# Normalising by halves of the time steps at each norm boundary, with the value tiles first in the key-value stage

## What is computed

```python
def rmsnorm(x, g):
    y = x * lax.rsqrt(jnp.mean(x * x, axis=-1, keepdims=True) + EPS)
    return y * g

x = x + short_conv_mixer(rmsnorm(x, mix_norm[0]), ...)   # stage a
x = x + conv_ffn(rmsnorm(x, ffn_norm[0]), ...)           # stage f0
kv = nsa_shared_kv(rmsnorm(x, kv_norm), ...)             # stage b
x = x + nsa_mixer(rmsnorm(x, mix_norm[1]), kv, ...)      # stage b
x = x + conv_ffn(rmsnorm(x, ffn_norm[1]), ...)           # stage f1
return rmsnorm(x, final_norm)                            # end
```

## Time and profile before

| | |
|---|---|
| median of 3 runs | 637.06 us |
| profiled execution | 636.12 us |
| its span, first to last instruction | 634.4 us |
| mean granted TensorE clock | 0.997 |
| busy: TensorE / VectorE / ScalarE / GpSimd | 97% / 77% / 63% / 8% |

### The profile page before, as it was taken

The page is one execution under the profiler, slowest core; times in us unless marked ns, Lnnn a source line. Parts: engine busy times, 40 slices in busy tenths (PEclk is TensorE's granted clock), DMA queues, the critical chain, the costliest instruction groups (busy, mean ns, idle before and its releaser), DMA issues.

```text
span 634.4 us, 11379 instructions
## 1 busy us (share of the span) xinstructions
PE 613.2 (97%) x3738; PEld 532.1 (84%) x3738; DVE 488.2 (77%) x1011; ACT 396.6 (63%) x764; POOL 53.7 (8%) x61
## 2 busy tenths in 40 slices
PE   7999999999999999999999888998999999999995
PEld 7999997888888888888989765777888888888884
DVE  4787656888888777777978799937788887777865
ACT  6645436666666566658555589827766666656644
POOL 0100011000000000011131143421000000000010
PEclk9999999999999999999999999999999999999998
DMA  8796432555655555761476300033455655555521
GB/s 304 303 334 240 168 132 100 194 204 198 201 198 198 197 179 185 295 204 41 154 247 212 123 2 2 2 100 132 136 205 197 217 205 191 177 174 189 198 100 67
DMA packets 30642, 109.56 MB, mean 173 GB/s; under 512 B 3419, under 2 KB 3691, under 8 KB 30476
## 3 DMA queue, kind: packets, MB, share of 16 engines
q1 hardware_dynamic: 30044, 106.97, 48.4%
q0 software_dynamic: 560, 2.12, 1.0%
HBM read 108.00 MB, written 1.07 MB: 172 GB/s over the span
## 4 chain that ended last, share of the span: by engine, by line
PE 88%; ACT 5%; DVE 3%; issue 2%; DMA 1%; POOL 0%; SPq 0%; DVEq 0%; ACTq 0%
PE bank L1059 26%; PE bank L1040 15%; PE bank L1041 14%; PE bank L1042 14%; PE bank L1060 13%; ACT work L667 2%; DMA staged<-in_a_up 1%; ACT w_hi L500 1%; DVE work L968 1%; ACT work L504 1%; PE bank L1264 1%; PE bank L1094 1%; PE bank L1306 1%; PE bank L1266 0%; ACT L479 0%
## 5 line engine op out<-in xcount | busy, mean ns | idle before, releaser
L714 DVE TENSOR_TENSOR w_lo<-staged,w_hi 128x1024 fp32r<-128x1024 f32 x191 | 236.8, 1248 | 41.9 <-ACT w_hi L500 41.8
L1059 PE MATMUL bank<-gx,w_hi 128*128 128x512 f32 x704 | 250.0, 398 | 0.9 <-DVE gx L788 0.9
L500 ACT ACTIVATE w_hi<-staged 128x1024 fp32r<-128x1024 f32 x197 | 199.7, 1046 | 25.3 <-PE bank L1042 15.7
L1060 PE MATMUL bank<-gx,w_lo 128*128 128x256 f32 x704 | 197.6, 281 | 0.0
L1059 PEld LDWEIGHTS bank<-gx,w_hi 128*128 128x128 f32 x704 | 132.2, 188 | 33.3 <-issue 1.3
L1060 PEld LDWEIGHTS bank<-gx,w_lo 128*128 128x128 f32 x704 | 133.0, 189 | 1.5
L1040 PE MATMUL bank<-w_hi,y 128*128 128x512 f32 x208 | 81.5, 392 | 0.0
L1041 PE MATMUL bank<-w_lo,y 128*128 128x512 f32 x208 | 81.5, 392 | 0.0
L1042 PE MATMUL bank<-w_hi,y 128*128 128x512 f32 x208 | 81.0, 389 | 0.0
L586 ACT ACTIVATE work<-work,params 128x256 f32<-128x256 f32 x96 | 44.2, 504 | 57.2 <-DVE work L815 39.2
L1040 PE MATMUL bank<-gx,w_hi 128*128 128x256 f32 x256 | 72.8, 284 | 2.8 <-DVE w_lo L714 2.4
(11 more groups left out here) (148 smaller groups left out, 799.5 us busy)
## 6 DMA issues: line engine op xcount, KB each, us to landing
staged<-in_f_up SPq DMA_DIRECT2D x88, 512.0 KB, 5.2
staged<-in_f_down SPq DMA_DIRECT2D x44, 512.0 KB, 3.3
staged<-in_a_up SPq DMA_DIRECT2D x24, 512.0 KB, 6.9
staged<-in_b_up SPq DMA_DIRECT2D x24, 512.0 KB, 4.3
staged<-in_a_down SPq DMA_DIRECT2D x8, 512.0 KB, 3.6
staged<-in_b_down SPq DMA_DIRECT2D x8, 512.0 KB, 4.3
bias<-bias_rows POOLq DMA_DIRECT2D x1, 2048.0 KB, 11.7
bias<-in_xT SPq DMA_DIRECT2D x4, 256.0 KB, 5.2
```

Of the source, the lines that this page charges most:

```text
L500: nc.scalar.activation(w_hi[:, q["slot"], 0:n], staged[:, s, 0:n], ACT.Copy).then_inc(hi, 1)
L714: nc.vector.tensor_tensor(w_lo[:, q["slot"], 0:n], staged[:, s, 0:n], w_hi[:, q["slot"], 0:n].bitcast(F32), ALU.subtract).then_inc(lo, 1)
L1059: nc.tensor.matmul(out_ap, w_hi[:, s, cols], gx[:, kt, :], start=start, stop=False, skip_group_check=True)
L1060: return nc.tensor.matmul(out_ap[:, 0:T], w_lo[:, s, cols], gx_hi[:, kt, :], start=False, stop=stop, skip_group_check=True)
```

## The change

- At every boundary the norm is made for time half 0 first and for half 1 after it, on all engines: residuals 0 and 1, two squares, root, scaling, eight transposes, high and low parts of 128 columns; then the rest. The matmuls on ones are removed.
- In f0 and f1, `units_0_1` takes the place of `unit_0` and `up_f(st, 1)`: the wide matmuls of units 0 and 1 are split into two matmuls of 2 x 128 columns each (`wide_half`), one for each time half; unit 0 and tile (1,0) are multiplied for half 0, then half 1 is transposed, and so on.
- In b the value tiles come first, half 0 of all four ahead of half 1; their products go to banks 0 and 1. Banks of cmp, key and q products move; tile numbers in ScalarE's order of b move with them.
- At the end of b, `last_projections` takes the last three output tiles by banks: both banks of half 0 for o5, o6 and o7, then bank 2, then bank 3. f1's first transposes stand behind o5's product for bank 3.
- Into f1, ScalarE copies tile (1,1) after the first half; (1,0) stays ahead of the norm.
- At the end, VectorE takes `half` 1 after the first pair of final products.

```diff
-B_ORDER = ([("cmp", t) for t in range(4)] + [("key", t) for t in range(4)] + [("val", t) for t in range(4)]
+B_ORDER = ([("val", t) for t in range(4)] + [("cmp", t) for t in range(4)] + [("key", t) for t in range(4)]
...
-KEEP_WARM = 5
...
-            return bank[b // 2 % 3][:, b % 2 * T:(b % 2 + 1) * T]
+            return bank[{2: 2, 3: 3, 4: 0, 5: 1}[b // 2]][:, b % 2 * T:(b % 2 + 1) * T]
...
+        def split_of(st, t, kt):
+            return 16 * NORM[st] - 8 + 8 * t + kt + 1
...
-            return bank[{0: 1, 1: 0, 2: 2}.get(t, 7)][:, 0:T]
+            return bank[{0: 2, 1: 4, 2: 5}.get(t, 7)][:, 0:T]
...
+                def squares_of(b):
...
                     act.wait_ge(x_new, 4 * (k - 1) + b + 1)
...
                     square(b // 2, slice(b % 2 * 512, b % 2 * 512 + 512), b)
...
+                def turned_half(t):
...
                     act.wait_ge(rstd_done, 2 * k + t)
                     nc.scalar.activation(xn[:, t, :, 3, :], x_parts[:, t, :, 3, :], ACT.Copy, scale=rstd_t[:, t:t + 1]).then_inc(xn_far, 1)
...
+                    cols = slice(t * P, t * P + P)
+                    for kt in range(KT):
+                        act.wait_ge(x_turned, 8 * (k - 1) + 4 * t + kt % 4 + 1)
+                        if kt >= 4:
+                            act.wait_ge(gx_lo_done, split_of(st, t, kt - 4))
+                        nc.scalar.activation(gx_hi[:, kt, cols], turned_x(st, kt)[:, cols], ACT.Copy,
+                                             scale=gain(GAIN_OF[st], kt)).then_inc(gx_hi_done, 1)
+                squares_of(0)
+                squares_of(1)
+                root(0)
+                if st == "end":
+                    squares_of(2)
+                    squares_of(3)
+                    root(1)
+                    return
+                turned_half(0)
+                if st == "f1":
+                    lead(*WHILE_O[-1])
+                squares_of(2)
+                squares_of(3)
+                root(1)
+                turned_half(1)
                 if st[0] == "f":
                     preload(ACT.Silu)
                 for n, q in enumerate(meanwhile):
                     lead(*q)
                     if st == "b" and n == 0:
-                        act.wait_ge(gx_lo_done, 8 * k + 8)
+                        act.wait_ge(gx_lo_done, split_of(st, 1, KT - 1))
...
+                if b in (6, 8):
...
+                if b in (10, 12):
...
-                        nc.scalar.activation(vals[:, k, :], bank[4 + k][:], ACT.Copy).then_inc(vals_done, 1)
+                        nc.scalar.activation(vals[:, k, :], bank[k][:], ACT.Copy).then_inc(vals_done, 1)
...
-            for q in WHILE_O:
+            for q in WHILE_O[:-1]:
                 lead(*q)
             norm("f1", meanwhile=SOON("f1"))
             stage("f1", [])
...
+                def scale(t):
                     inverse(st, t)
...
                     for c in range(3):
                         nc.vector.tensor_scalar(xn[:, t, :, c, :], x_parts[:, t, :, c, :], rstd_t[:, t:t + 1], None, ALU.mult).then_inc(xn_done, 1)
...
+                def rests(t):
+                    cols = slice(t * P, t * P + P)
+                    for kt in range(KT):
+                        dve.wait_ge(gx_hi_done, split_of(st, t, kt))
+                        nc.vector.scalar_tensor_tensor(gx_lo[:, kt, cols], turned_x(st, kt)[:, cols], gain(GAIN_OF[st], kt),
+                                                       gx_hi[:, kt, cols].bitcast(F32), ALU.mult, ALU.subtract).then_inc(gx_lo_done, 1)
...
+                residual(st, 0)
+                residual(st, 1)
+                half(st, 0)
                 if st == "end":
+                    residual(st, 2)
+                    residual(st, 3)
+                    inverse(st, 0)
+                    dve.wait_ge(final_landed, 16)
+                    finals(0)
+                    half(st, 1)
+                    inverse(st, 1)
+                    finals(1)
                     return
-                for kt in range(KT):
-                    dve.wait_ge(gx_hi_done, 8 * k + kt + 1)
-                    nc.vector.scalar_tensor_tensor(gx_lo[:, kt, :], turned_x(st, kt), gain(GAIN_OF[st], kt),
-                                                   gx_hi[:, kt, :].bitcast(F32), ALU.mult, ALU.subtract).then_inc(gx_lo_done, 1)
+                if st == "f1":
+                    scale(0)
+                    residual(st, 2)
+                    rests(0)
+                    residual(st, 3)
+                else:
+                    residual(st, 2)
+                    scale(0)
+                    residual(st, 3)
+                    rests(0)
+                half(st, 1)
+                scale(1)
+                rests(1)
...
+            def turn_x(st, t):
...
-                pe.wait_ge(x_new, 4 * (k - 1) + 1)
-                for n in range(KEEP_WARM):
-                    nc.tensor.matmul(bank[ACC_BEFORE[st]][:, 0:P], ones[:], ones[:], start=True, stop=True)
...
+                if t:
+                    pe.wait_ge(gx_lo_done, split_of(st, 0, KT - 1))
+                for c in range(4):
+                    if c == 3:
+                        pe.wait_ge(xn_far, 2 * (k - 1) + t + 1)
+                    else:
+                        pe.wait_ge(xn_done, 6 * (k - 1) + 3 * t + c + 1)
+                    for a in range(2):
+                        mm = nc.tensor.transpose(turned_x(st, 4 * a + c)[:, t * P:t * P + P], xn[:, t, a, c, :], ident[:])
+                    mm.then_inc(x_turned, 1)
+            def wide_half(st, k, c, t, kt):
+                out_ap, x_ap = (ap.rearrange("p (a t) -> p a t", a=2)[:, :, t * P:t * P + P]
+                                for ap in (bank[UP[st] + 2 * k + c], gx[:, kt, :]))
+                s = piece_of(st, "up", k, c)["slot"]
+                nc.tensor.matmul(out_ap, w_hi[:, s, kt * P:kt * P + P], x_ap, start=t == 0 and kt == 0, stop=False,
+                                 skip_group_check=True)
+            def narrow(st, k, c):
+                s = piece_of(st, "up", k, c)["slot"]
+                for kt in range(KT):
+                    mm = nc.tensor.matmul(bank[UP[st] + 2 * k + c][:, 0:T], w_lo[:, s, kt * P:kt * P + P], gx_hi[:, kt, :],
+                                          start=False, stop=kt == KT - 1, skip_group_check=True)
+                mm.then_inc(used_up, 1)
+            def units_0_1(st):
+                def split_up(k, c):
+                    pe.wait_ge(lo_up, piece_of(st, "up", k, c)["n"] + 1)
+                split_up(0, 0)
+                split_up(0, 1)
+                for kt in range(KT):
+                    pe.wait_ge(gx_lo_done, split_of(st, 0, kt))
+                    for c in range(2):
+                        wide_half(st, 0, c, 0, kt)
+                pe.wait_ge(x_new, 4 * NORM[st])
+                split_up(1, 0)
+                for kt in range(KT):
+                    wide_half(st, 1, 0, 0, kt)
+                turn_x(st, 1)
+                split_up(1, 1)
+                for kt in range(KT):
+                    wide_half(st, 1, 1, 0, kt)
+                for kt in range(KT):
+                    pe.wait_ge(gx_lo_done, split_of(st, 1, kt))
+                    for c in range(2):
+                        wide_half(st, 0, c, 1, kt)
                 for c in range(2):
...
+                    narrow(st, 0, c)
+                for c in range(2):
+                    for kt in range(KT):
+                        wide_half(st, 1, c, 1, kt)
+                    narrow(st, 1, c)
+            def values(tt):
+                for t in range(4):
+                    q = piece_of("b", "up", B_ORDER.index(("val", t)), 0)
                     pe.wait_ge(lo_up, q["n"] + 1)
-                for kt in range(KT):
-                    if j == 0:
-                        pe.wait_ge(gx_lo_done, 8 * NORM["b"] + kt + 1)
-                    for b, q in enumerate(todo):
-                        s = q["slot"]
-                        mm = three(pair_bank(2 * j + b), w_hi[:, s, kt * P:kt * P + P], w_lo[:, s, kt * P:kt * P + P], gx_hi[:, kt, :],
-                                   gx_lo[:, kt, :], b == 0 and kt == 0, kt == KT - 1)
-                        if kt == KT - 1:
-                            mm.then_inc(used_up, 1)
+                    if tt == 0 and t == 3:
+                        turn_x("b", 1)
+                    for kk in range(2):
+                        kt = 2 * t + kk
+                        pe.wait_ge(gx_lo_done, split_of("b", tt, kt))
+                        mm = three(bank[tt][:], gx_hi[:, kt, tt * P:tt * P + P], gx_lo[:, kt, tt * P:tt * P + P],
+                                   w_hi[:, q["slot"], kk * 512:kk * 512 + 512], w_lo[:, q["slot"], kk * 512:kk * 512 + 512],
+                                   kt == 0, kt == KT - 1)
+                    if tt == 1:
+                        mm.then_inc(used_up, 1)
...
+                    if st == "f0":
+                        turn_x(st, 0)
+                    units_0_1(st)
```

(54 more changed lines are left out.)

65 lines of the change are left out of this document (7 added, 58 removed).

## The result

The kernel after takes 641.97 us (median of 4 runs, 640.82 to 642.21), beside 636.76 for the kernel before (4 runs, 636.34 to 637.26) on the same chip: 1.0078 times as long, 95% interval 1.0066 to 1.0090. It is slower by 0.8%, clear of noise. Its profiled execution took 642.21, with a span of 640.5 against 634.4. Every median and ratio in this document is over executions of the usual speed; two of the twelve of the kernel with split products, at 761.0 and 866.65 us with a mean granted clock of 0.75 and 0.65, are left out.

What follows compares the result with a forecast made beforehand. TensorE, busy 97% of the span, was taken to bound the kernel, so only four norm boundaries matter. Terms -0.1 - 0.1 + 3.0 + 0.45 + 1.2 = +4.45 gave 640.6 us profiled, 641.5 median; range 638.3 to 643.4.

Steps and rivals of the forecast that it cites:

- Into f1, +3.0: Boundary into f1: o5's slot released 4.07 us later delays copy, norm and transposes; TensorE idles 5.4; +3.0 us.
- the price of splitting: Wide products in f0 and f1: two halves cost as much as the whole; bound nothing to 0.3 us for 64 halves.
- The clock, +1.2: Into f1: the granted clock falls during the 5.4 us wait, slowing work after it; +1.2 us, bounds nothing and 1.7.
- Rival B: Into f1: the clock stays up through the 5.4 us wait; +3.25 in all, 640.3 us; chance 0.24.
- The drain: Into f1, Sqrt table switch: taken without drain; the skill's 2.66 us would put the first square at 440.2, sum 0.7 higher.
- Into f0, -0.1: Boundary into f0: first product 1.5 us earlier, but the gain given back around the second half; -0.1 us.
- The thin cover: In f0, VectorE's sum for unit 0 frees banks at 117.9, unit 2 wants them at 118.0; costed at nothing, else 0.5.
- Into b, -0.1: Boundary into b: -0.5 us from an earlier start, +0.4 from waiting for cmp 1's low part; -0.1, bounds -0.5 and +0.8.
- Rival C: Thin covers fail too: both waits for unit 2 (1.0) and the compression block (0.8); 643.3 us; chance 0.08.
- D: At the boundaries, high and low parts in halves cost half the whole (0.19 and 0.20), clock up; +1.85, 638.9 us; chance 0.12.
- The end, +0.45: At the end, half, root and inverse come after the first pair of products, delaying the second pair; +0.45 us onto the output.
- Rival E: Into f1: the first turn hides under the last projections, f1 giving -3.3; 634.0 us; chance 0.08.

Runs made afterwards that it cites:

- kernel with split products: The kernel before with the wide products of units 0 and 1 in f0 and f1 each split in two, no halves of the norm: 637.74 us, ratio 1.0009.
- run with ones: The kernel after with 20 matmuls on ones in the wait ahead of f1's first transposes: 640.26 us, ratio 1.0046 against the kernel before.
- copy moved: The kernel after with f1's tile (1,0) copied behind the first half's high parts, its low part behind residual 3: 636.77 us, ratio 0.9996 against the kernel before.
- o5 released first: The kernel after with o5 multiplied whole ahead of o6 and o7, f1's first turn behind them all: 636.90 us, ratio 0.9993 against the kernel before.
- old projections: The kernel after with the last three output tiles taken whole as before, f1's first turn behind them: 638.05 us, ratio 1.0017 against the kernel before.

## Why the prediction was right

**The outcome and the size.** Forecast 641.5, measured 641.97; of the terms, +4.45, measured +4.86 without the start. The sum is nearer than its parts: f0 came out 0.41 above its term and f1 with the clock 0.33 above, b 0.21 and the end 0.15 below.

**Into f1, +3.0: right in mechanism and in nearly all of its size.** Less the 1.27 by which this profile runs late, the copy of (1,0) into o5's slot starts at 436.52 (said: 436.5), the low part at 437.61 (437.6), the first square at 439.46 (439.55), the root at 440.83 (440.9), the first transpose at 441.76 (441.8), and the wait is 5.34 (5.4). With the clock up it cost 3.31. The step that was short is the price of splitting: I put nothing on it, with a bound of 0.3. In f1 of the split kernel it was 0.22 against the profile of before, and 0.54 against the same program with whole products at their faster pace. The second turn, at 448.1 on the clock of before in the run with ones (449.60 less 1.46, by which its last pair of head matmuls is later), was also 0.4 later than said.

**The clock, +1.2: right.** 1.22, by the run with ones. Rival B, a clock that stays up, falls with the windows of the kernel after. One reading on which I chose was wrong: 1.5 is not the longest wait that left the clock up, since in the kernel before it stayed at 1.00 through stage a's 2.4. And 3.1 is no fixed delay: at the end of the ten profiles the clock fell 2.2 to 5.3 us after the last matmul ended, and into f1 after 3.8. A wait of 5.4 could be taken to let it fall, but with less margin than I gave: the longest of those delays, 5.3, is that of the kernel with split products.

**The drain.** The table load takes 1.28, and the small activation behind it starts 1.30 after the load's start; the first square then waits 0.37 for VectorE's residual. By the 2.66 us of the Trainium skill (ScalarE: Activation LUTs, "What ACT_TABLE_LOAD costs"), load and drain, it would stand at 441.5, an estimate from that page; it stands at 440.73. The trace does not show the drain, here as in the earlier trace rows.

**Into f0, -0.1: wrong in sign, +0.31.** The landmarks held: first product 2.95 after the last down matmul (said 3.1), the second turn waited for 0.29, the high and low parts of 128 columns pace at 0.27 each. The step that failed is "I put no cost on its splitting", and its bound of 0.3 was too low: in the kernel before the same 32 split products cost 0.43, and 0.55 with unit 2 behind them. Without that the halves would have won 0.24 here. Unit 2 did not wait: VectorE's sum of unit 0 was issued at 118.56, and the product came at 119.58 behind TensorE's own work. The thin cover held, with some 0.3 left.

**Into b, -0.1: -0.31.** The second turn started without a wait. The late cmp 1 did come: of the two L1084 waits shown above, 3.3 in all, 3.1 is stage a's, and the other 0.2 is cmp 1 behind its low part, where I had taken 0.4; `gq_lo`, the step ahead of it, came at 304.70 on before's time rather than 304.95. Next late, as named, was the compression block: GpSimd's residue ended at 330.52 and w1 0 started at 330.92, unhindered. Rival C falls. So does D: the halves cost 0.27 on both engines, as in the terms.

**The end, +0.45: +0.30.** The second pair starts 3.42 after the last matmul instead of 3.13. The first pair came 0.28 earlier and not 0.1; that is the difference.

**Rival E.** It was to decide at one point, whether the squares start before o5's release. They did not. With the copy moved or o5 released first, the first turn hid as E has it; but head to last fell by at most 1.4, not by the 3.3 that E gave: it left out the new wait at the second turn, unit 2's and the pacing.

**What was not in the sum.** The profile of after lost 1.24 in stage a, with a lower clock from 11.4 to 14.8 us. Three of the four executions of the kernel after have the lower mean clock. The forecast of the median was near the mark although this was not thought of; that much of it is luck.

## What to carry to other kernels

When an order of work is changed, write down which buffers each new order releases later, and who stands behind them in an in-order queue: here a release 4 us later, for a copy that was not needed yet, cost more than everything that the change could hide. Work by halves moves the wait to the second half unless the engines are free by then; cost the second half's chain as carefully as the first's, and put a price on every instruction that is split. Look at what a neighbour engine has running when the chain needs VectorE: a GpSimd subtraction of 2.4 us held the scaling back by up to 0.9. Before crediting a hidden boundary, ask whether the wait that stays lets the clock fall.

## What the runs showed of the hardware

- The clock fell 3.8 us after TensorE's last work into f1, and 2.2 to 5.3 us after the last matmul at the end of the ten profiles; stage a's wait of 2.4 left it up in the kernel before.
- The granted clock fell after a stretch of light work in which no wait was over 1.5 us (copy moved: busy 0.49, 0.69, 0.00 and 0.81 of four successive us). A stretch nearly as light, with o5 released first, did not make it fall:

```profile
443.00:444.00 1.00, 0.82 (x8) 1.00 0.00 0
444.00:445.00 1.00, 0.00 (x0) 1.00 0.00 0
445.00:446.00 1.00, 0.81 (x7) 1.00 0.00 0
```

- VectorE's scaling of three blocks took 1.74 beside a GpSimd subtraction of 128 x 1024, and 0.88 without it. It was held rather than slowed: in four profiles where the scaling starts during the subtraction (copy moved, old projections, o5 first, after), its first instruction ends 0.15 or 0.16 after the subtraction does, and the other two take 0.34 each.
- A matmul of 512 columns and its two strided halves differ by 7 to 13 ns per product, depending on which of two paces (0.347 or 0.353 us a product) the whole ones have; 32 products make it 0.2 to 0.4 us. Both paces occur in f1 of the same program.
- ScalarE's and VectorE's copies from PSUM took 0.27 each at 128 columns (eight in 2.19 and 2.16 in f0 of the kernel after) and 0.38 and 0.40 at 256.
